# Forty-four more unread products of the identity on TensorE, at eleven places of one decoder step

## What is computed

```python
# every sub-layer: x <- LayerNorm(ALPHA * x + f(x))
# layer 0: sliding-window attention (window 128) and retention side by side, one input and one output projection
qa, ka, va, qr, kr, vr, g = even_project(x, pos, w_in)
x = ln(ALPHA * x + even_output(swa(qa, ka, va), retention(qr, kr, vr), g, w_out))
# layer 1: latent attention in its place
# both layers: cross attention into 256 memory tokens, then the experts
x = ln(ALPHA * x + mem_attend(x, mk, mv, w_q, w_o))
# experts: group of 4 by argmax, top 2 of its 4 experts, SwiGLU of width 256
logits = x @ w_group + b_group, x @ w_router + b_router
x = ln(ALPHA * x + sum(gate * (silu(a) * b) @ w_out[e]))
```

## Time and profile before

| | us |
|---|---|
| median of 3 runs | 1016.05 |
| the three runs | 1021.74, 1015.88, 1016.05 |
| the profiled execution, device time | 1021.6 |
| its span, first to last instruction | 1019.8 |
| PE busy in the span | 961.7 (94%) |
| DVE busy | 510.5 (50%) |
| ACT busy | 353.7 (35%) |
| POOL busy | 245.9 (24%) |
| share of PE in the chain that ended last | 73% |
| mean granted TensorE clock | 0.969 |

### The profile page before, as it was taken

How to read it: one execution, slowest core, us unless ns; L and a number is a source line. 1 busy time by engine, 2 the same in 40 slices (tenths; PEclk the granted TensorE clock), 3 DMA queues, 4 the chain that set the end, 5 groups by cost and what they waited for, 6 DMA issues and landing times.

```text
span 1019.8 us, 17897 instructions
## 1 busy us (share of the span) xinstructions
PE 961.7 (94%) x7032; PEld 592.7 (58%) x7032; DVE 510.5 (50%) x1068; ACT 353.7 (35%) x891; POOL 245.9 (24%) x291
## 2 busy tenths in 40 slices
PE   7999999999998998799999999999999988999995
PEld 6876787878544856533333666657658664333332
DVE  0245630365838758532222374566768783333227
ACT  3335442020102345133333364355314442343323
POOL 3550000051500002345410014510000025552121
PEclk9999999979999999799999999899999978999999
DMA  9736100172203463889999812423167156999978
GB/s 318 199 88 235 58 1 9 75 207 83 73 0 74 139 256 118 305 327 409 416 414 414 322 58 57 94 66 131 42 207 290 42 210 223 353 417 414 417 220 202
DMA packets 78059, 203.61 MB, mean 200 GB/s; under 512 B 19128, under 2 KB 44384, under 8 KB 68880
## 3 DMA queue, kind: packets, MB, share of 16 engines
q1 hardware_dynamic: 61568, 153.44, 41.2%
q0 software_dynamic: 16400, 48.93, 15.4%
HBM read 184.46 MB, written 25.92 MB: 206 GB/s over the span
## 4 chain that ended last, share of the span: by engine, by line
PE 73%; DVE 12%; DMA 8%; ACT 4%; issue 2%; POOL 1%; SPq 0%; DVEq 0%; POOLq 0%; ACTq 0%
PE PS L1663 14%; PE PS L1450 10%; PE PS L1091 8%; PE PS L1197 6%; PE PS L1680 6%; PE PS L1481 3%; DMA x<-y_tok 2%; PE PS L1063 2%; PE PS L1651 2%; ACT arena L2095 2%; DMA ring<-in_moe_w_in_dram 2%; DMA arena<-in_moe_w_in_dram 2%; PE PS L1158 1%; PE PS L1075 1%; PE PS L1829 1%
## 5 line engine op out<-in xcount | busy, mean ns | idle before, releaser
L1663 PE MATMUL PS<-ring,arena 128*32 128x512 f32 x696 | 137.6, 592 | 0.4 <-DMA ring<-in_moe_w_in_dram 0.2
L2095 ACT ACTIVATE arena<-PS 32x520 f32<-32x520 f32 (+9 forms) x138 | 69.4, 514 | 171.7 <-PE PS L1091 40.4
L1663 PE MATMUL PS<-arena 128*32 128x512 f32 x600 | 106.8, 593 | 1.7 <-issue 1.7
L1091 PE MATMUL PS<-xT,ring 128*128 128x260 f32 x416 | 95.2, 390 | 4.2 <-DVE arena L2596 3.1
L3196 DVE COPY arena<-PS 128x256 f32<-128x256 f32 x24 | 10.2, 425 | 173.4 <-PE PS L1671 173.4
L1091 PEld LDWEIGHTS PS<-xT,ring 128*128 128x128 f32 x416 | 79.5, 193 | 19.1 <-DVE arena L2596 5.1
L2394 ACT ACTIVATE arena<-PS,lnc 128x128 f32<-128x128 f32 x184 | 66.8, 468 | 36.4 <-PE PS L1651 36.4
L1663 PEld LDWEIGHTS PS<-ring,arena 128*32 128x32 f32 x696 | 37.0, 110 | 55.0 <-issue 51.0
L1680 PE MATMUL PS<-ring,arena 128*32 128x512 f32 x408 | 65.4, 595 | 0.6 <-DVE arena L3196 0.6
L1197 PE MATMUL PS<-ring,xT 128*128 128x256 f32 (+2 forms) x336 | 65.2, 354 | 0.0
L889 POOL DMA_INDIRECT y_tok<-arena,slot_dest x22 | 22.3, 1012 | 166.1 <-ACT arena L2432 157.3
(11 more groups left out here) (448 smaller groups left out, 1834.6 us busy)
## 6 DMA issues: line engine op xcount, KB each, us to landing
ring<-in_moe_w_in_dram SPq DMA_DIRECT2D x29, 1024.0 KB
arena<-in_moe_w_in_dram SPq DMA_DIRECT2D x25, 1024.0 KB
ring<-in_moe_w_out_dram SPq DMA_DIRECT2D x17, 1024.0 KB
ring<-in_w_in_even_dram SPq DMA_DIRECT2D x11, 1024.0 KB
xT<-in_moe_w_in_dram SPq DMA_DIRECT2D x10, 1024.0 KB, 12.2
arena<-in_moe_w_out_dram SPq DMA_DIRECT2D x9, 1024.0 KB
xT<-in_moe_w_out_dram SPq DMA_DIRECT2D x6, 1024.0 KB, 16.9
y_tok<-in_c_zeros_dram POOLq DMA_DIRECT2D x8, 512.0 KB, 10.8
```

What stands on the lines that cost most here:

```text
L1091: mm = pe.matmul(o[out_rows, 512 * h:512 * h + HALF], lhs(k), rhs(k)[:, HALF * h:HALF * h + HALF], start=(k == 0), stop=(k == nk - 1))
L1663: mm = pe.matmul(o[group(q), 0:512], xT_[:, k, group(q)], w(q, k), start=(k == 0), stop=(k == KD - 1), **quarter(q))
L2095: return act.activation(dst, src, ACT.Copy)
```

## The change

Products are added at these places, and nothing else is touched:

| where | products added | columns | position in TensorE's order |
|---|---|---|---|
| sliding attention, ahead of qr.3 | 4 | 128 | ahead of `open_`, into the pair of swaO.0 |
| retO.0 | 5 | 128 | behind `open_` |
| x.1 and x.2 of the first memory stage | 2 and 3 | 128 | behind `open_`, ahead of the wait for `normed` |
| sO, sOt | 3 and 2 | 128 | behind `open_` |
| first transposes of layer 1, xT(2, 0) | 5 | 128 | behind `open_`, ahead of the wait for `normed` |
| lg.1, rt.0, in both layers | 4 and 2 each | 128 | behind `open_` |
| table, in both layers | 3 become 5, and 1 + 1 more behind block_sums(0) and block_table(0) | 256 | behind `open_` |

The four products ahead of x's last tile (x of stages 1 and 4) stay as they are; they come from the table `TURN_UNREAD` now.

```diff
+TURN_UNREAD = {(0, 1): 2, (0, 2): 3, (1, NT - 1): 4, (4, NT - 1): 4, (2, 0): 5}
@@ transpose_x
-                if i % 3 == 1 and t == NT - 1:
-                    unread_products(o[:, 896:1024], 4)
+                unread_products(o[:, 896:1024], TURN_UNREAD.get((i, t), 0))
                 pe.wait_ge(x_in[t], 16) if i < 0 else wait_normed(pe, i, t)
@@ sliding attention
             def between(n):
+                if n == 2:
+                    unread_products(pair(att_key("swa", "O", 0))[:, 896:1024], 4)
                 for key in SWA_WEAVE[n]:
                     project(key)
@@ retention
                 key = ("retO", n)
                 o = open_(key)
+                if n == 0:
+                    unread_products(o[:, 896:1024], 5)
                 taken(pe, ("retS", n))
@@ state_output
                 o = open_(key)
+                unread_products(o[:, 896:1024], 3)
                 taken(pe, ("sU", 3))
@@ state_output_back
                 o = open_(key)
+                unread_products(o[:, 896:1024], 2)
                 taken(pe, ("sO",))
@@ logits
                     pe.wait_ge(s["wr_zero"], 1)
+                    if t == 1:
+                        unread_products(o[:, 896:1024], 4)
                     taken(pe, ("xT", 3 * l + 1, t))
@@ logits_back
+                    if t == 0:
+                        unread_products(o[:, 896:1024], 2)
                     taken(pe, ("lg", l, t))
@@ experts, table
-                unread_products(o[:, 768:1024], 3, routes)
+                unread_products(o[:, 768:1024], 5, routes)
...
                 block_sums(0, "dest_sums")
+                unread_products(o[:, 768:1024], 1, routes)
                 pe.wait_ge(s["dest_rows"], l + 1)
                 block_table(0).then_inc(s["dest_table"], 1)
+                unread_products(o[:, 768:1024], 1, routes)
                 pe.wait_ge(s["gates_ready"], l + 1)
```

## The result

| | median | runs | profiled execution: span, clock |
|---|---|---|---|
| before, measured beside it | 1018.65 us | 1012.63 to 1025.04 (15) | 1019.8 us, 0.969 |
| after | 1025.24 us | 1021.73 to 1030.81 (15) | 1024.7 us, 0.976 |

A forecast was written before the change was run, and what follows sets the result against it. TensorE, 94% busy, bounds the kernel, slowed by a 0.969 mean clock. Terms -1.7, -3.3, -1.0, +1.2, -1.3 sum to -6.1: 1015.5 us from 1021.6, or 1010.0 if low runs lack other stretches; 1011 taken, range 1003 to 1018.

The forecast's parts named there:

- the boundary's: Layer 1's first transposes: five products come after a code-fetch pause, costing 1.2 us (2.0 at half clock), with no gain.
- the front part: Sliding attention, retention and first memory stage together: slow stretches avoided, -1.7, -3.3 and -1.0 us.
- The rule quoted there: Layer boundary: a taken branch out of the fetched window stalls the engine for a code transfer, supporting the +1.2 us.
- Sliding attention, -1.7: Ahead of qr.3: four products fill 0.98 of a 1.85 us wait at no cost, winning back the slow stretch's 1.7 us.
- Retention, -3.3: At retO.0: five products behind the wait cost 1.2 us but avoid a 10 us slow stretch worth 4.5 us.
- Memory stage, -1.0: At x.1, sO, x.2 and sOt: products cost 0.4 us and avoid a slow stretch worth 1.4 us.
- lg.1 and rt.0: In each router: lg.1's four products cost 0 to 0.2 us, rt.0's two 0.5 us (0.8 at half clock).
- Routers, -1.3: Both routers: half of a countable 4.6 us won, -2.3, plus 2 x 0.5 for rt.0.
- The base: Starting time: profiled 1021.6 us is a long run, 1016.05 a low one; the difference was read as slow stretches only some runs have.
- rival 2: Whole kernel: slow stretches move rather than vanish; only sliding attention gains, products cost 3.8 us, time 1018; 0.22 with rival 4.
- Rival 3: At the added products: they run at half clock behind pauses they do not fill, costing 8.4 us, time 1024.5; chance 0.06.
- Rival 4: Experts: transfers of their weights hold the gain back, time 1015; chance 0.22 together with rival 2.

The follow-up runs named there:

- part 4: Parts of the change tried singly on the kernel before, code position held; its table compares stretch times with and without the products: layer 0's router 69.1 for 67.4 us.
- a_pad: Changed kernel with 37 products written into the never-run spill body, putting the branch's target at 92 modulo 256: 0.9999 of the kernel before.
- c_mid: Changed kernel without the boundary's products, 224 more instructions in the never-run body, target at 168 modulo 256: 0.9979 of the kernel before.
- e_late: Changed kernel without the boundary's products, target at 200; SP requests expert rows of tiles 2 to 4 only after x's first tile is turned: 0.9997 of before.
- f_late2: Changed kernel without boundary's products, eight ahead of the first block's gather wait, target at 92, rows of tiles 2 to 4 requested late: 0.9988 of before.

## Why the prediction was wrong

The time lies 7 us above the range of 1003 to 1018. By the steps of the prediction:

- **The step that failed** is the boundary's. It saw the pause of 2.21 us, read it as the fetch of code behind the passed-over `If`, and put the products behind it: all right (2.14 us, then the products; alone they measured +1.2 us, the forecast's own figure). But it priced only what stands behind the branch, and not what the 110 instructions added ahead of it do: they move the branch's target within its stretch of code. That is +5.4 us, shown in both directions (5.4 to 7.6 in three pairs), and no rival had it. The statement that "nothing else is touched" held for the work, not for where it stands. It is about half of the miss of some 10 us. With the code held the change measured 0.9999 (0.9977 to 1.0021), so the forecast of 5 us faster would have missed without it too, by the terms of the front part (-2.8 in the traces, -4.0 measured, for -6.0) and of the routers.
- The rule quoted there (the Trainium skill, Runtime: NRT & Kernel Launch, Instruction fetch mechanics) also says that code comes in blocks of 256 instructions, fetched in sequence while the current one runs. The traces agree with both halves: the second pause moved by 32 instructions when 224 were added, and lasted 1.4 us with 42 instructions left for 3.1 with 10. It gives no duration; here the next block was there after 3.0 us with idle transfers and after 4.2 to 6.0 with full ones.
- **Sliding attention, -1.7:** right in the trace (-1.7, clock 1.00 from 86 to 97 us, the products ahead of qr.3), but the slow stretch that it removes was absent in two of five profiles of the same code.
- **Retention, -3.3:** the mechanism was right. Ten records stand behind DVE's end, 1.38 us for the 1.2 counted, and chunk 1's sixteen take 1.71 us for 3.09. In the trace it gave -2.9. Mis-sized was the assumption that every execution has that slow stretch: where it is absent the products cost the 1.2, and alone the part measured -1.2.
- **Memory stage, -1.0:** -1.7 in the pair of traces; sOt takes 1.89 us for 3.25. This slow stretch too is absent in three of the five.
- **lg.1 and rt.0:** right. The waits of 0.17 and 0.85 us take up lg.1's 1.16, and from ACT's last copy to rt's products it is 4.8 us for 4.3, the 0.5 of rt.0's own.
- **Routers, -1.3:** alone -2.0 with an interval from -4.7 to +0.6, but in the table of part 4 +1.7 in layer 0 and -0.1 in layer 1. What the sum missed is the gather behind the table of layer 0, which a sooner table only turns into idle time (2.49 us) with a slow stretch behind it; and in layer 1 the slow clock fell from 18.2 to 4.9 us without a gain in time. Why not is not shown.
- **The base.** I took low and high runs of before for executions with and without slow stretches. That much is so: of the 35 runs beside a_pad, those under 1017 us have a clock of 0.974 to 0.978 and those above 1024 us 0.966 to 0.969. But I reached 1011 from a sum against one profile, with nearly every stretch of it taken for one that executions always have, and in five profiles the slow time ahead of 395 us ranges from 3.4 to 17.0 us. And 1016.05 was a median of three runs; fifteen beside the changed kernel gave 1018.65. With the code held, the whole change is 0.9999, near rival 2 (the slow stretches move, 1018); a_pad and c_mid show some of it, with slow stretches at 251 to 258 us, where before had none. That the number came so near is in part luck: rival 2 has neither the executions in which the front part is fast anyway nor the wait for the gather.
- **Rival 3**, the one on the slow side, gave 1024.5, and the time came out at 1025.2, by another mechanism. The products at half clock cost 0.8 to 0.9 us more at the boundary (1.99 us for ten records in a_pad, 0.71 and 1.44 in after, for the 1.2 at full clock). **Rival 4** named the weights; the runs with less of them and after's wait of 0.5 us speak against it.

What is open: why layer 1's router is no faster with so much less slow clock, what the boundary's products cost (1.2 or 3.4 us), and whether the longer slow stretch of latent attention in after (13.7 us for 6.8) is more than chance; the profiles of other kernels had 3.4 to 13.7 there.

## What to carry to other kernels

Code that is jumped over has a price that moves with every instruction added ahead of it: where a long body is passed, look for idle time without a releaser behind its end, and again some instructions later. Before an edit of unrelated work is judged, hold the target's place by padding the body that isn't run, and compare with that. A slow stretch of the clock in one profiled execution is a chance, not a price: take its share over several profiles before counting it as a gain, and set against it what the cure costs the executions that don't have it.

## What the runs showed of the hardware

- Behind the jump over the spill body TensorE stood idle for 2.1 to 2.7 us while the transfers were full (the profiles of eighteen kernels), and the fetch was hidden altogether where they were nearly empty (e_late, f_late2).
- A packet of code (16 KB) took 0.9 to 1.1 us at the layer boundary, with the transfers full or empty, and TensorE went on 1.5 to 1.6 us behind its end. With full transfers it started 1.7 to 3.4 us behind TensorE's first instruction, with empty ones 0.5 us.
- If the stretch of code ended some ten instructions behind the target, TensorE stood idle for 3.1 to 5.3 us more (2.3 with empty transfers), with 42 instructions left 1.4, with 118 none. Moving the code alone changed the time by 0.5% in either direction.
- The same list of instructions had from 3.4 to 17.0 us of slow clock in its first 395 us, in five executions.
- Slow clock that goes away is not always time that is won: in layer 1's router it fell from 18.2 to 4.9 us (means of six and seven executions), and the stretch took 75.4 us for 75.5.
